# First mixer of an fp32 block pair: index turns and gate moved inside the key/query tiles, low parts on one engine, head squares on ScalarE

## What is computed

```python
def mixer_ab(n, pos, w_in, gq, gk, w_gate_up, b_gate, g_gla, w_out):
    proj = n @ w_in
    (qa, ka, va, iq, ik, iw, qb, kb, vb, g_low, og) = _split(proj, AB_SIZES)
    qa = rope_partial(rmsnorm(qa.reshape(bsz, s_len, N_HEADS_A, HEAD_DIM), gq), pos)
    ka = rope_partial(rmsnorm(ka.reshape(bsz, s_len, N_HEADS_A, HEAD_DIM), gk), pos)
    iq = rope_partial(iq.reshape(bsz, s_len, IDX_HEADS, IDX_DIM), pos)
    ik = rope_partial(ik[:, :, None, :], pos)[:, :, 0, :]
    oa = dsa_attention(qa, ka, va, iq, ik, iw).reshape(bsz, s_len, A_WIDTH)
    gate = (g_low @ w_gate_up + b_gate).astype(jnp.float32)
    lg = (jax.nn.log_sigmoid(gate) / GLA_TAU).reshape(bsz, s_len, N_HEADS_B, GLA_DK)
    ob = gla_chunked(qb, kb, vb, lg).astype(n.dtype)
    ob = rmsnorm(ob, g_gla).reshape(bsz, s_len, B_WIDTH) * jax.nn.silu(og)
    return jnp.concatenate([oa, ob], axis=-1) @ w_out
```

## Time and profile before

| | |
|---|---|
| time, median of 3 runs | 1040.65 us (1039.6 to 1041.95) |
| profiled execution | 1041.85 us, its span 1040.0 us |
| mean granted TensorE clock | 0.981 of full |
| TensorE matmul busy | 1001.5 us, 96% of the span |
| weight loads busy | 898.7 us, 86% |
| VectorE / ScalarE / GpSimd busy | 582.4 / 523.7 / 415.7 us |
| bytes read from HBM | 166.77 MB, 161 GB/s |

### The profile page before, as it was taken

The page is one execution under the profiler, slowest core; times in us unless marked ns, Lnnn a source line. Parts: engine busy times, 40 slices in busy tenths (PEclk is TensorE's granted clock), DMA queues, the critical chain, the costliest instruction groups (busy, mean ns, idle before and its releaser), DMA issues.

```text
span 1040.0 us, 15063 instructions
## 1 busy us (share of the span) xinstructions
PE 1001.5 (96%) x6334; PEld 898.7 (86%) x6334; DVE 582.4 (56%) x798; ACT 523.7 (50%) x684; POOL 415.7 (40%) x129
## 2 busy tenths in 40 slices
PE   7979999999999999899999999999998989999997
PEld 6867788999888888779999888899898879999885
DVE  4688784888522445526787312444127277888643
ACT  6444445454433566646554333645443466566442
POOL 2433315656566563435565766355434400000000
PEclk9989899999999999999999999999999989999999
DMA  8424305445555543424545555444334425454541
GB/s 322 160 96 169 140 1 203 163 174 192 202 178 189 198 164 122 145 102 164 200 168 198 189 178 199 159 173 179 122 122 162 162 85 180 170 195 176 189 162 41
DMA packets 24787, 168.78 MB, mean 162 GB/s; under 512 B 2784, under 2 KB 3056, under 8 KB 4880
## 3 DMA queue, kind: packets, MB, share of 16 engines
q1 hardware_dynamic: 24432, 167.49, 45.4%
q10 hardware_dynamic: 288, 0.33, 0.1%
HBM read 166.77 MB, written 1.05 MB: 161 GB/s over the span
## 4 chain that ended last, share of the span: by engine, by line
PE 85%; DVE 8%; ACT 5%; issue 1%; DMA 1%; SPq 0%; DVEq 0%; ACTq 0%
PE bank L609 26%; PE bank L610 25%; PE bank L611 25%; ACT whi L1048 2%; PE bank L798 2%; DVE wlo L1581 1%; PE bank L991 1%; PE bank L1007 1%; DVE a L1693 1%; PE bank L636 1%; DVE a L1661 1%; DMA h<-x_rows 1%; PE bank L979 1%; DVE a L1708 1%; DVE b L2065 1%
## 5 line engine op out<-in xcount | busy, mean ns | idle before, releaser
L2162 POOL TENSOR_TENSOR wlo<-raw,whi 128x1024 fp32r<-128x1024 f32 (+1 forms) x123 | 414.8, 3375 | 411.3 <-ACT whi L1048 411.0
L1581 DVE TENSOR_TENSOR wlo<-raw,whi 128x1024 fp32r<-128x1024 f32 (+2 forms) x154 | 230.2, 1495 | 343.7 <-ACT whi L1048 343.7
L1048 ACT ACTIVATE whi<-raw 128x2048 fp32r<-128x2048 f32 (+1 forms) x154 | 292.4, 1901 | 148.1 <-PE bank L611 147.0
L609 PE MATMUL bank<-nhi,whi 128*128 128x258 f32 (+3 forms) x1160 | 332.0, 286 | 3.8 <-DVE nlo L2086 2.5
L610 PE MATMUL bank<-nlo,whi 128*128 128x258 f32 (+3 forms) x1160 | 329.5, 284 | 0.0
L611 PE MATMUL bank<-nhi,wlo 128*128 128x258 f32 (+3 forms) x1160 | 328.1, 283 | 0.0
L609 PEld LDWEIGHTS bank<-nhi,whi 128*128 128x128 f32 (+1 forms) x1160 | 220.8, 190 | 8.3 <-issue 8.1
L611 PEld LDWEIGHTS bank<-nhi,wlo 128*128 128x128 f32 (+1 forms) x1160 | 221.4, 191 | 0.0
L610 PEld LDWEIGHTS bank<-nlo,whi 128*128 128x128 f32 (+1 forms) x1160 | 221.2, 191 | 0.1
L609 PE MATMUL bank<-whi,nhi 128*128 128x512 f32 x192 | 81.1, 422 | 5.7 <-POOL wlo L2162 5.7
L610 PE MATMUL bank<-wlo,nhi 128*128 128x512 f32 x192 | 78.1, 407 | 0.0
(11 more groups left out here) (261 smaller groups left out, 1424.8 us busy)
## 6 DMA issues: line engine op xcount, KB each, us to landing
raw<-w_stream SPq DMA_DIRECT2D x154, 1024.0 KB, 4.8
cst<-consts SPq DMA_DIRECT2D x1, 1200.0 KB, 11.7
h<-x_rows SPq DMA_DIRECT2D x4, 256.0 KB, 5.4
raw<-w_stream SPq DMA_DIRECT2D x2, 512.0 KB, 6.5
out_rows<-e SPq DMA_DIRECT2D x4, 256.0 KB, 2.0
b<-consts_x SPq DMA_DIRECT2D x1, 544.0 KB, 5.6
e<-g_post SPq DMA_DIRECT2D x1, 512.0 KB, 3.3
raw<-w_stream SPq DMA_DIRECT2D x1, 352.0 KB, 9.3
```

Source lines behind the costliest of these rows:

```text
L609: pe.matmul(out, lhsT.hi, rhs.hi, start=start, stop=False)
L1048: act.activation(whi[j][:, 0:n], raw[j][:, 0:n], ACT.Copy).then_inc(s_hi.up(i))
L1581: dve.tensor_tensor(wlo[j][:, 0:m], raw[j][:, 0:m], whi[j][:, 0:m].bitcast(F32), ALU.subtract).then_inc(s_lod.up(i))
L2162: pool.tensor_tensor(wlo[j][:, m:n], raw[j][:, m:n], whi[j][:, m:n].bitcast(F32), ALU.subtract).then_inc(s_lop.up(i))
```

## The change

It reorders the first mixer and moves four kinds of work.

- Gate product and key turn stand between the two halves of QB, the index turns between the two halves of KB. Index scores 0 to 3 stand before `proj(1)`, 4 to 7 between its tiles. The bank plan follows: `gate` is taken before `qkb` 1.
- `cut(i)` says how many columns of a low part VectorE makes: all for tiles below 17 and from 125 on, none for tiles 10 and 12, half for the rest. GpSimd makes the remainder, and waits before tile 12 for the rope of attention queries and keys (`s_ropea`).
- ScalarE's order is changed: the gate's softplus ahead of `hi(6)`, and `hi(7)` to `hi(14)` at other places among levels, scores and head norms.
- In `head_norms` ScalarE squares the four heads one by one with an accumulated sum; VectorE's reduce is gone.
- VectorE drains `qkb` 0 behind the index rope and `qkb` 1 behind `lo(6)`; levels, scores, `best`, rope and `lo` are put in another order. GpSimd's fill of `SEL` comes first.

```diff
+def cut(i):
+    n = tile_sizes()[i]
+    if i in (10, 12):
+        return 0
+    return n if i < OUT_AB + 2 or i >= UP2 + 2 else n // 2
...
-    proj(1, [("sc", n) for n in range(4)])
-    for n in range(4, 8):
+    for n in range(4):
         banks.take("sc", n)
+    proj(1, [("sc", n) for n in range(4, 8)])
...
             for j in range(2):
-                w, u = weights(QB + j, 8), begin("qkb", j)
+                w, qk = weights(QB + j, 8), begin("qkb", j)
                 weights_in(QB + j)
                 for p in range(2):
                     for k in range(8):
-                        x = mm3(u.t[:, p * 256:p * 256 + 256], w[:, k, p * P:p * P + P], nTa[:, k, :], k == 0, k == 7)
-                x.then_inc(u.full)
+                        x = mm3(qk.t[:, p * 256:p * 256 + 256], w[:, k, p * P:p * P + P], nTa[:, k, :], k == 0, k == 7)
+                    if p == 0:
+                        (key_turn, index_turn)[j]()
+                x.then_inc(qk.full)
...
-            proj(1, 0, lambda: scores(0, 4))
-            scores(4, 8)
+            scores(0, 4)
+            proj(1, 0, lambda: scores(4, 8))
```

In ScalarE's `head_norms`:

```diff
-                    act.activation(q, u.t[:, :].rearrange("p (h d) -> p h d", h=4), ACT.Square, scale=rs[:, tt:tt + 1]).then_inc(s_qsq.up(j, tt))
-                    on.wait_ge(*s_qss.at(j, tt))
+                    for hd in range(4):
+                        act.activation(q[:, hd, :], u.t[:, hd * P:hd * P + P], ACT.Square, scale=rs[:, tt:tt + 1],
+                                       accum_out=ssA[:, j, tt, hd:hd + 1]).then_inc(own.up())
+                    on.wait_ge(*own.last())
```

In ScalarE's order:

```diff
-            levels(0, 3)
+            levels(0, 2)
+            scores(0, 4)
             hi(7)
-            scores(0, 4)
+            levels(2, 3)
+            scores(4, 6)
             hi(8)
+            scores(6, 8)
             head_norms(0)
-            scores(4, 8)
+            hi(9)
             levels(3, 4)
-            hi(9)
             hi(10)
...
-            levels(4, 5)
             hi(13)
...
-            levels(5, 7)
+            levels(4, 6)
             hi(14)
-            levels(7, 8)
+            levels(6, 8)
```

In VectorE's order:

```diff
-            levels(0, 3)
+            level_diff(0)
+            level_diff(1)
+            lo(6)
+            branch(1)
+            level_scale(0)
+            scores(0, 4)
+            level_diff(2)
+            level_scale(1)
             lo(7)
-            scores(0, 4)
+            scores(4, 8)
             lo(8)
             head_norms(0)
-            scores(4, 8)
-            levels(3, 4)
+            level_diff(3)
+            level_scale(2)
             lo(9)
             best(0, 4)
-            lo(10)
             head_norms(1)
             lo(11)
+            on.wait_ge(*s_qg.at(1, 1))
+            rope(QA, 8, 16, "cosA", "sinA", s_ropea)
             best(4, 8)
```

In GpSimd's program:

```diff
-            for i in range(2, ALONE):
+            for i in range(2, NTILE):
+                j, m, n = i % NSLOT, cuts[i], sizes[i]
+                if m == n:
+                    continue
                 on.wait_ge(*s_hi.at(i))
+                if i == 12:
+                    on.wait_ge(*s_ropea.at(1))
                 pool.tensor_tensor(wlo[j][:, m:n], raw[j][:, m:n], whi[j][:, m:n].bitcast(F32), ALU.subtract).then_inc(s_lop.up(i))
```

More of the change, by code:

```diff
@@ L299, in plan_banks @@
     banks.take("keyT")
+    banks.take("gate")
     banks.take("qkb", 1)
     last[KB] = (("qkb", 1), 0)
-    banks.take("gate")
     for n in range(2):
@@ L574, in block_kernel @@
         s_rl, s_sc = sig("rl", range(8)), sig("sc", grid(8, 2))
-        s_qsq, s_qss, s_qrs, s_qg = (sig(n, grid(2, 2)) for n in ("qsq", "qss", "qrs", "qg"))
+        s_qrs, s_qg = sig("qrs", grid(2, 2)), sig("qg", grid(2, 2))
         s_am0, s_sel0, s_sel, s_ropea = sig("am0", [0]), sig("sel0", [0]), sig("sel", range(2)), sig("ropea", range(2))
@@ L725, in tensor_program, with key_turn, index_turn @@
             x.then_inc(u.full)
-            for j in range(2):
-                if j == 1:
-                    u = begin("keyT")
-                    on.wait_ge(*use["keys",].gone())
-                    for tt in range(2):
-                        x = pe.transpose(u.t[:, tt * 88:tt * 88 + 88], GL[0:88, tt * P:tt * P + P], ident[0:88, 0:88])
-                    x.then_inc(u.full)
-                w, u = weights(QB + j, 8), begin("qkb", j)
+            def key_turn():
+                u = begin("keyT")
+                on.wait_ge(*use["keys",].gone())
+                for tt in range(2):
+                    x = pe.transpose(u.t[:, tt * 88:tt * 88 + 88], GL[0:88, tt * P:tt * P + P], ident[0:88, 0:88])
+                x.then_inc(u.full)
+                u = begin("gate")
+                for p in range(2):
+                    x = pe.matmul(u.t[:, p * 256:p * 256 + 256], wg[:, p * P:p * P + P], GL[0:16, :], start=True, stop=True)
+                x.then_inc(u.full)
+            def index_turn():
+                for tt in range(2):
+                    u = begin("iqT", tt)
+                    on.wait_ge(*s_ropei.at(1))
+                    for m in range(4):
+                        x = pe.transpose(u.t[:, m * P:m * P + P], IQ[:, tt * 576 + m * P:tt * 576 + m * P + P], ident)
+                    x.then_inc(u.full)
+                u = begin("ikT")
+                on.wait_ge(*s_ikd.at(3))
+                for tt in range(2):
+                    x = pe.transpose(u.t[:, tt * P:tt * P + P], IKD[:, tt * P:tt * P + P], ident)
+                x.then_inc(u.full)
+            for j in range(2):
+                w, qk = weights(QB + j, 8), begin("qkb", j)
                 weights_in(QB + j)
@@ L1629, in vector_program, with branch @@
             dve.tensor_tensor(GL[0:88, :], u.t[0:88, 0:256], RSB[0:88, :], ALU.mult).then_inc(u.free)
-            for j in range(2):
-                lo(5 + j)
+            def branch(j):
                 u = use["qkb", j]
@@ L1668, in level_scale @@
                 for j, side in ((0, 1), (1, 0)):
+                    on.wait_ge(*use["qkb", j].gone())
                     ov = QKE[:, l, :].rearrange("p (b u s) -> p b u s", u=2, s=hs)[:, :, side, :]
@@ L1671, in level_scale @@
                     dve.tensor_tensor(ov, iv, dv[:, :, side, :], ALU.mult).then_inc(s_lvq.up(l, j))
-            def levels(lo_, hi_):
-                for l in range(lo_, hi_):
-                    level_diff(l)
-                    if l:
-                        level_scale(l - 1)
             def scores(lo_, hi_):
@@ L1740, in vector_program @@
                 dve.tensor_scalar(SELv[:, tt, 0:P * (tt + 1)], wks[tt], -2.0e38, BIGNEG, ALU.is_gt, ALU.mult).then_inc(s_sel.up(tt))
-            lo(12)
-            on.wait_ge(*s_qg.at(1, 1))
-            rope(QA, 8, 16, "cosA", "sinA", s_ropea)
-            levels(4, 5)
             lo(13)
-            levels(5, 7)
+            level_diff(4)
+            level_scale(3)
+            level_diff(5)
+            level_scale(4)
             lo(14)
-            levels(7, 8)
+            level_diff(6)
+            level_scale(5)
+            level_diff(7)
+            level_scale(6)
             level_scale(7)
```

48 lines of the change are left out of this document (15 added, 33 removed).

## The result

The changed kernel takes 1022.43 us (median of 4 executions, 1021.88 to 1022.84), the kernel before in the same series 1040.37 (1039.6 to 1041.95). The ratio is 0.9825, its 95% interval 0.9808 to 0.9842: 17.9 us faster, where 16.0 was forecast. The profiled execution took 1022.84 us, its span is 1021.0 us, the mean granted clock 0.993 (before: 1041.85, 1040.0, 0.981).

A forecast was written before the change was run, and what follows sets the result against it. TensorE, busy 96%, was taken as the bound, so gains come from gaps and low clock: 16.4 us less 0.4 of VectorE lag gives 16.0, from 1040.65 to 1024.7 us. The 8-in-10 range was 1022.7 to 1031.

The forecast's parts named there:

- What bounds the kernel, and what there is to win: First mixer's projections, 26 to 120 us: TensorE's waits and the low clock after them cost 16.4 us, all winnable.
- Why the waits were there: Split low parts: GpSimd's half takes 3.43 us and can hold VectorE's two-input instructions about 2.1 us, three times.
- The new order, by instruction lists: All engines from 26.3 us on: no TensorE wait left, thinnest margin 0.5 us, first `gla_1` at 95.7.
- Squares by ScalarE: Head norms: four 128-column squares with accumulator take 1.7 us, with Ln and Exp 2.35 us per token half.
- my balance: VectorE's load in the changed stretch: 8.5 - 2.4 - 6.3 - 2.7 = -2.9 us, the reduces being the 2.7.
- What comes due next: Behind the first `gla_1`: VectorE reaches `att_1` only 16.1 us earlier, near 107.6; 0.4 us comes off the gain.
- The lower end of the range: Whole kernel: 1022.7 us, the time at full catch-up less 0.1% of run-to-run.
- full catch-up: Rival for the mixer: gaps and clock losses gone, VectorE catches up fully, 16.9 us, 1023.8; inside the forecast's 0.62.
- A: Tile 9: GpSimd's tile 10 reads first, `lo(9)` is held; 5.4 us lost, 1030.0; chance 0.24.
- B: First mixer: one serial chain through VectorE and ScalarE, TensorE waits elsewhere; gain at most 2.9 us, 1037.7; chance 0.08.
- the high parts by free slot: ScalarE: `hi(7)` no longer waits behind level 2, nor `hi(9)` behind `levels(3, 4)`; tile 9's slot was free at 56.4.
- C: Tiles 9 and 12: GpSimd's two 4.7 us instructions hold VectorE's two-input work; 6.5 us slower, 1047.2; chance 0.06.

The follow-up runs named there:

- the repeats: The changed kernel run again unaltered, twice, against the kernel before: 1025.02 us (first repeat) and 1022.95 us (second).
- undo_squares: The changed kernel with one 512-column Square on ScalarE and VectorE's reduce put back: 1028.74 us, ratio 0.9886 to the kernel before.

## Why the prediction was right or wrong

**What bounds the kernel, and what there is to win: right.** The sum of waits and clock losses was 16.4 us; with every wait gone and the clock at 1.00, the changed stretch gave 16.65, and 16.63 and 16.62 in the repeats.

**Why the waits were there: right,** and shown twice: the products held from 0.75 to 2.97 us when the split is put back, the low part held from 2.28 to 5.68 when GpSimd gets ahead of it.

**The new order, by instruction lists: right to 0.8 us, and to about 0.5 once the 0.46 us of the earlier start are added to the measured times.** Forecast against measured, as the profile has them: end of `lo(6)` 39.75 and 39.45, `lo(7)` 49.9 and 49.6, `lo(8)` 56.5 and 56.5, `lo(9)` 62.9 and 62.7, GpSimd's tile 10 from 62.9 to 67.6 and from 62.95 to 67.6, `lo(11)` 72.7 and 72.6, rope 74.9 and 74.8, GpSimd's tile 12 from 74.9 to 79.6 and 74.93 to 79.57, `lo(13)` 82.3 and 82.2, `lo(14)` 90.9 and 90.3, last level 94.5 and 93.9, first `gla_1` 95.7 and 95.22, first `att_1` 107.6 and 106.8.

**Squares by ScalarE: right in size, wrong in what they are worth.** 1.7 us per token half were taken for the four squares; they repeat every 0.34 us and need 1.54 to the logarithm. But my balance counted the reduces only as 2.7 us of VectorE's load. What they hold up is ScalarE: 3.75 and 1.50 us of standing in the first pair of head norms, 5.16 in the second, whose high part TensorE then waits for. This did not enter the sum, since the order by lists already had ScalarE free of it; it did make my expectation for `undo_squares` fall short, 1022 to 1023.5 for 1028.74.

**What comes due next: this term was wrong, by 0.4 us and more.** I took 0.4 off for VectorE's lag behind `gla_1`. VectorE reached its first `att_1` 16.9 us earlier, not 16.1 (16.46 without the start's share), and the changed stretch shows no such loss: 16.65 against 16.0. With the 0.46 us of an earlier full speed at the start, which no edit made, the mixer gave 17.1.

**The lower end of the range: this is the step that failed, by its size.** It was the gain of full catch-up, 16.9 us, less 0.1% (1.0 us) "of run-to-run". The 16.9 itself is 0.5 above the sum of 16.4 that was called all there is to win, and no row shows these 0.5; the changed stretch gave 16.65. The 0.1% was far too little: all stages ahead of and behind the changed stretch were taken as merely shifted. They are shifted, but what TensorE does there at full and at half speed differs between executions. In three profiles of the changed kernel the row factors start at 21.61 to 22.63 us, and from the mixer's end on identical instructions take 887.85 to 890.0; twelve executions spread over 4.2 us. The first series lay low in that spread (1022.43), the other two (1025.02 and 1022.95) inside the range. The starting point adds its share: the range was reckoned from 1040.65, and the kernel before took 1040.37 beside the changed one, 0.28 us less, as much as the range was missed by. So it is luck of the draw that the first series fell outside; what the range lacked is the spread of the start and of the later gaps, 1.0 and 2.2 us in those three profiles. The forecast of 1024.7 is 1.4 above the mean of the twelve, 1023.3: 0.65 us of that is the changed stretch, the rest lies in the start and the later gaps, which I did not split further.

**The rivals.** A did not occur: `lo(9)` started at 60.45, 2.5 us ahead of GpSimd's 62.95, where 2.1 were forecast. Moving one instruction brought it about, at 1030.6 against A's 1030.0. B (the stage is one serial chain) is refuted by the empty list of waits. It has a true core, though: each part undone alone makes the changed stretch longer by 6.4 (low parts), 4.4 (squares) and 7.6 us (turns), and the low parts alone, without the rest, did nothing for the longest wait, because another queue still ended it. How the gain divides among the parts stays open: the three add up to 18.4, more than the whole 16.65, so they overlap, and the fourth part, the high parts by free slot, was not undone by itself. C (GpSimd's long instructions on VectorE's path) did not occur.

## What to carry to other kernels

Lay the instruction lists of all engines against each other with measured durations, and find for each wait the queue that is late at its root. A part that shortens only the last link (the low parts alone) leaves the wait as long as it was. A short step that sends an engine to another's queue and back costs what stands in that queue, not its own duration. And when stages behind the change hold gaps, take the spread of several series of the same kernel for the range, not that of three executions. To see what a change is worth below that spread, measure the changed stretch alone between two marks: here it agreed to 0.03 us in three traces whose totals differed by more than a microsecond.

## What the runs showed of the hardware that was not expected

- The clock after one and the same wait of 2.87 us of TensorE differs between executions of one kernel: granted 1.00 or 0.70 in the 5 us around it; with it a 512-column product takes 0.39 or 0.63 us. In twelve traces the wait was followed by no loss (three) or by one of 1.6 to 1.7 us (nine), nothing in between.
- At the start of the kernel the first products of the weights take 0.63 us, and the change to 0.39 comes at 11.3, 13.1 or 14.0 us in three executions (first repeat, after, before), while the granted clock of that stretch reads 1.00; there only the durations tell the speed. With early throwaway products they take 0.39 to 0.50 from the first on.
- A 2048-column difference of two SBUF tensors on VectorE takes 2.28 us, and 5.68 when GpSimd's own (4.58) began a microsecond before it. MAX8 and MATCH_REPLACE8 beside the same GpSimd instruction keep 0.61 a pair and 0.27.
- A Square of 128 columns with its sum accumulated repeats every 0.34 us on ScalarE although its two rows are 0.37 and 0.20 long: the read lies half within the activation. For 256 columns the two add up to 0.69.
